# A gate table from one f32r product a token, with its copies and one-hot tiles moved between engines

## The reference

```
u = u_emb[ids]
act = gelu(einsum('ted,td->te', u, xb))
w = gate * act
out = einsum('te,ted->td', w, v_emb[ids])
```

## Time and profile before

| | us |
|---|---|
| median of 3 runs | 3590.15 |
| lowest and highest | 3589.37, 3594.89 |
| the profiled execution's own time | 3598.26 |
| its span in the trace | 3596.5 |

### The profile page before, as it was taken

One profiled execution on the slowest core, in us unless ns is written; L12 is line 12 of the kernel. 1 busy time (PEld: TensorE's weight loads), 2 busy tenths in 40 slices (PEclk: granted clock), 3 DMA queues, 4 the chain that ended last, 5 costly groups with the idle time before them and its releaser, 6 DMA issues. The chain is left out here.

```text
span 3596.5 us, 52641 instructions
## 1 busy us (share of the span) xinstructions
PE 3509.6 (98%) x19484; PEld 2990.6 (83%) x19484; DVE 1772.6 (49%) x3403; ACT 1283.5 (36%) x1851; POOL 500.7 (14%) x428
## 2 busy tenths in 40 slices
PE   8999999999999999999999999999999999899999
PEld 8966787788888878888888899998889789768887
DVE  7344599566665224444444543335445456654333
ACT  4244222466665232222222322233223333333232
POOL 0100125433332001111111010010100000111011
PEclk9989999999999999999999999999999989999999
DMA  4200224355555546666666422222222100122221
GB/s 148 77 18 18 88 95 140 123 175 175 178 181 184 190 144 190 194 189 193 190 193 197 129 88 94 82 94 74 91 85 77 59 1 1 36 76 97 93 99 69
DMA packets 115447, 416.05 MB, mean 116 GB/s; under 512 B 14192, under 2 KB 14320, under 8 KB 113008
## 3 DMA queue, kind: packets, MB, share of 16 engines
q1 hardware_dynamic: 75632, 279.93, 23.6%
q0 software_dynamic: 18944, 67.12, 6.4%
q10 hardware_dynamic: 20736, 67.12, 5.0%
HBM read 344.91 MB, written 69.21 MB: 115 GB/s over the span
## 5 line engine op out<-in xcount | busy, mean ns | idle before, releaser
L447 DVE TENSOR_TENSOR w_lo<-ring,w_hi 128x1024 fp32r<-128x1024 f32 x224 | 275.4, 1230 | 698.0 <-ACT w_hi L443 698.0
L183 DVE TENSOR_TENSOR w_lo<-ring,w_hi 128x1024 fp32r<-128x1024 f32 (+2 forms) x157 | 205.9, 1311 | 568.7 <-ACT w_hi L177 568.7
L443 ACT ACTIVATE w_hi<-ring 128x1024 fp32r<-128x1024 f32 x255 | 270.2, 1059 | 505.9 <-PE ps L493 488.8
L463 PE MATMUL ps<-hn_hi,w_hi 128*128 128x512 f32 x1024 | 408.1, 398 | 3.6 <-POOL w_lo L447 1.4
L463 PE MATMUL ps<-hn_lo,w_hi 128*128 128x512 f32 x1024 | 404.5, 395 | 0.0
L463 PE MATMUL ps<-hn_hi,w_lo 128*128 128x512 f32 x1024 | 402.9, 393 | 0.0
L493 PE MATMUL ps<-units_hi,w_hi 128*128 128x512 f32 x1024 | 399.1, 390 | 2.7 <-DVE units_lo L804 2.7
L493 PE MATMUL ps<-units_hi,w_lo 128*128 128x512 f32 x1024 | 399.0, 390 | 0.0
L493 PE MATMUL ps<-units_lo,w_hi 128*128 128x512 f32 x1024 | 398.9, 390 | 0.0
L177 ACT ACTIVATE w_hi<-ring 128x1024 fp32r<-128x1024 f32 (+2 forms) x170 | 190.2, 1119 | 455.0 <-PE ps L241 381.0
L241 PE MATMUL ps<-f_hn_hi,w_hi 128*128 128x264 f32 (+1 forms) x1056 | 284.6, 324 | 8.9 <-DVE f_hn_lo L855 8.5
(11 more groups left out here) (432 smaller groups left out, 6723.6 us busy)
## 6 DMA issues: line engine op xcount, KB each, us to landing
ring<-in_w_uv SPq DMA_DIRECT2D x256, 512.0 KB, 3.4
ring<-in_f_up SPq DMA_DIRECT2D x88, 512.0 KB, 3.2
expert_units<-scratch ACTq DMA_DIRECT2D x128, 256.0 KB, 2.6
gate_table<-peer ACTq DMA_DIRECT2D x16, 2048.0 KB, 7.2
peer<-gate_table POOLq DMA_DIRECT2D x32, 1024.0 KB, 8.0
peer<-expert_units POOLq DMA_DIRECT2D x128, 256.0 KB, 3.7
ring<-in_w_in SPq DMA_DIRECT2D x29, 512.0 KB, 3.3
ring<-in_w_late SPq DMA_DIRECT2D x25, 512.0 KB, 3.3
```

Of the source, the lines that this page charges most:

```text
L183: self.nc.vector.tensor_tensor(self.l[:, self.slot(k), 0:self.cols], e.ring[:, self.ring(k), 0:self.cols], self.h[:, self.slot(k), 0:self. ...
L443: A_(uh[:, slot(n)], e.ring[:, ring(n), 0:D], ACT.Copy).then_inc(e.hi_done, 1)
L447: ops.tensor_tensor(ul[:, slot(n)], e.ring[:, ring(n), 0:D], uh[:, slot(n)].bitcast(F32), ALU.subtract).then_inc(e.lo_done, 1)
L463: mm = M(e.ps[:, n % 2, :], u[:, slot(n), ch * P:(ch + 1) * P], x[part][:, ch, META:L], start=(ch == 0 and j == 0), stop=(ch == DC - 1 and ...
```

## The change

- **Products.** A token's product becomes one f32r matmul of 256 columns: the moving tile holds the row scaled by the gate's high part and by its low part, side by side. A batch takes two PSUM banks, and two batches alternate (`both`).
- **Rows.** VectorE makes the moving tile by one `scalar_tensor_tensor` of 256 elements a token, from iota, the token's row as a pointer scalar, and the pair of gate parts. It keeps four batches of them.
- **Columns.** GpSimd's `offset` subtracts for every batch; ScalarE's `columns` does Abs and Relu, in place, for every batch, 512 elements each.
- **Evacuation.** ScalarE's `high` copies the half from the high parts out of PSUM, contiguously; VectorE's new `evac` adds the other half from PSUM and writes the transposed table.
- **Order.** `hi` and `lo` are done for unit n+2 in step n. ScalarE: `columns` twice, `gelu`, `spill`, `hi`, `high` twice, and the save every fourth time. VectorE: `hots` for the next step's two batches, `lo`, `evac` twice. In the units 96 to 127, `hi` and `lo` run two ahead as well.
- Once, at the start, the gates are split into their parts. The tiles lie where they did; `tb.high` takes two scratch rows.

```
-    hot, hot_pool, hot_act = e.sem("hot"), e.sem("hot_pool"), e.sem("hot_act")
+    hot, hot_col = e.sem("hot"), e.sem("hot_col")
+    parted, copied = e.sem("gate_parts"), e.sem("high_copied")
...
+    def both(m):
+
+        at = (4 + 2 * (m % 2)) * WIDE
+        return e.psf[:, at:at + 2 * WIDE].rearrange("p (t x i) -> p t x i", t=GT, x=2)
+
...
         def outers(it, m):
 
-            r = m % GR
             pe.wait_ge(hot, it * 16 + (m + 1))
-            if r % 2 == 0:
-                pe.wait_ge(hot_pool, it * 8 + (m // 2 + 1))
-            if r % 4 == 1:
-                pe.wait_ge(hot_act, it * 4 + (m // 4 + 1))
+            pe.wait_ge(hot_col, it * 16 + (m + 1))
             pe.wait_ge(stored, it * 16 + (m + 1))
             for t in range(GT):
-                mm = M(e.ps[:, 4 + m % 4, t * P:(t + 1) * P], tb.cols[:, r, t], tb.rows[:, r, t])
+                mm = M(both(m)[:, t].rearrange("p x i -> p (x i)"), tb.cols[:, m % GR, t],
+                       tb.rows[:, m % 4, t].rearrange("p x i -> p (x i)"))
             mm.then_inc(outer, 1)
...
-        act.sem_inc(stored, 4)
...
         def columns(it, m):
 
-            act.wait_ge(outer, it * 16 + (m + 1))
-            for t in range(GT):
-                col = it * (16 * GT) + (m * GT + t)
-                off = A_(tb.cols[:, m % GR, t], c["iota"], ACT.Abs, bias=e.colT[:, bass.ds(col, 1)], scale=-1.0)
-            off.then_inc(act_offset, 1)
-            act.wait_ge(act_offset, it * 4 + (m // 4 + 1))
-            A_(tb.cols[:, m % GR], tb.cols[:, m % GR], ACT.Relu, bias=e.one, scale=-1.0).then_inc(hot_act, 1)
-
-        def evac(it, m):
-
-            blk = m // BK
-            if m % BK == 0:
-                act.wait_ge(saved[blk], it * 16 + 16)
+            x = tb.cols[:, m % GR]
+            act.wait_ge(pool_offset, it * 16 + (m + 1))
+            A_(x, x.bitcast(F32), ACT.Abs).then_inc(act_offset, 1)
+            act.wait_ge(act_offset, it * 16 + (m + 1))
+            A_(x, x.bitcast(F32), ACT.Relu, bias=e.one, scale=-1.0).then_inc(hot_col, 1)
+
+        def high(it, m):
+
             act.wait_ge(outer, it * 16 + (m + GR + 1))
-            t0 = (m % BK) * GT
-            A_(tb.table[:, blk].rearrange("p i t -> p t i")[:, t0:t0 + GT, :],
-               e.ps[:, 4 + m % 4, :].rearrange("p (t i) -> p t i", t=GT), ACT.Copy).then_inc(stored, 1)
+            A_(tb.high[m % 2], both(m)[:, :, 0], ACT.Copy).then_inc(copied, 1)
 
         def save(it, blk):
 
-            act.wait_ge(stored, it * 16 + (BK * (blk + 1) + 4))
+            act.wait_ge(stored, it * 16 + (BK * (blk + 1) + 2))
             act.dma_start(e.gtab[it * 2 + blk],
                           tb.table[:, blk].rearrange("p i t -> p (i t)")).then_inc(saved[blk], 16)
...
             for j, y in enumerate((e.rowT, e.colT, e.gateT)):
-                cp = A_(y[:, n * P:(n + 1) * P], e.ps[:, 4 + n, j * P:(j + 1) * P], ACT.Copy)
-            cp.then_inc(spread, 1)
+                A_(y[:, n * P:(n + 1) * P], e.ps[:, 4 + n, j * P:(j + 1) * P], ACT.Copy)
+            A_(tb.gates[:, n * P:(n + 1) * P, 0], e.ps[:, 4 + n, 2 * P:3 * P], ACT.Copy).then_inc(spread, 1)
 
         act.wait_ge(spread, nb)
-        columns(0, 1)
-        columns(0, 5)
+        hi(act, 0, 8, AHEAD + 1)
+        for m in range(4):
+            columns(0, m)
 
         def table_step(it, n, more):
-            hi(act, it, 8, AHEAD + n + 1)
+            if more:
+                columns(it, 2 * n + 4)
+                columns(it, 2 * n + 5)
             gelu(it, 8, AHEAD + n)
             spill(it, 8, AHEAD + n - 1)
-            evac(it, 2 * n)
-            evac(it, 2 * n + 1)
-            if n % 2 == 0 and more:
-                columns(it, 2 * n + 1 + GR)
+            hi(act, it, 8, AHEAD + n + 2)
+            high(it, 2 * n)
+            high(it, 2 * n + 1)
             if n % 4 == 3:
                 save(it, n // 4)
 
...
         for n in range(8):
-            table_step(SPREAD // 8 - 1, n, n < 4)
-        with act.Fori(0, REST // 4) as it:
+            table_step(SPREAD // 8 - 1, n, n < 6)
+        with act.Fori(0, REST // 4 - 1) as it:
             for n in range(AHEAD + SPREAD, AHEAD + SPREAD + 4):
-                hi(act, it, 4, n + 1)
                 gelu(it, 4, n)
+                hi(act, it, 4, n + 2)
                 spill(it, 4, n - 1)
+        for n in range(NK - 4, NK):
+            gelu(0, 4, n)
+            if n < NK - 1:
+                hi(act, 0, 4, n + 2)
+            spill(0, 4, n - 1)
         spill(0, 4, NK - 1)
 
...
-        def offset(it, j):
-
-            pool.wait_ge(outer, it * GR + (2 * j + 1))
-            if not isinstance(it, int) or j:
-
-                pool.wait_ge(pool_offset, it * (GR // 2) + j)
-            col = it * (GR * GT) + 2 * j * GT
-            nc.gpsimd.tensor_tensor(tb.cols[:, 2 * j % GR], c["iota"].unsqueeze(1).broadcast_to([P, GT, P]),
-                                    e.colT[:, bass.ds(col, GT)].unsqueeze(2).broadcast_to([P, GT, P]),
+        def offset(it, m):
+
+            pool.wait_ge(outer, it * GR + (m + 1))
+            nc.gpsimd.tensor_tensor(tb.cols[:, m], c["iota"].unsqueeze(1).broadcast_to([P, GT, P]),
+                                    e.colT[:, bass.ds(it * (GR * GT) + m * GT, GT)].unsqueeze(2).broadcast_to([P, GT, P]),
                                     ALU.subtract).then_inc(pool_offset, 1)
 
-        def equal(j):
-            nc.gpsimd.tensor_scalar(tb.cols[:, 2 * j], tb.cols[:, 2 * j], 0.0, None,
-                                    ALU.is_equal).then_inc(hot_pool, 1)
-
-        turns = batches // GR
         pool.wait_ge(spread, nb)
+        with pool.Fori(0, batches // GR) as it:
+            for m in range(GR):
+                offset(it, m)
...
         def hots(it, m):
 
-            r = m % GR
-            dve.wait_ge(outer, it * 16 + (m + 1))
+            dve.wait_ge(outer, it * 16 + (m + GR - 4 + 1))
             for t in range(GT):
                 col = it * (16 * GT) + (m * GT + t)
-                oh = V.tensor_scalar(tb.rows[:, r, t], c["iota"], e.rowT[:, bass.ds(col, 1)],
-                                     e.gateT[:, bass.ds(col, 1)], ALU.is_equal, ALU.mult)
-                if r % 4 == 3:
-                    oh = V.tensor_scalar(tb.cols[:, r, t], c["iota"], e.colT[:, bass.ds(col, 1)], None,
-                                         ALU.is_equal)
+                parts = tb.gates[:, bass.ds(col, 1)].bitcast(F32).rearrange("p o x -> p (o x)")
+                oh = V.scalar_tensor_tensor(out=tb.rows[:, m % 4, t],
+                                            in0=c["iota"].unsqueeze(1).broadcast_to([P, 2, P]),
+                                            scalar=e.rowT[:, bass.ds(col, 1)],
+                                            in1=parts.unsqueeze(2).broadcast_to([P, 2, P]),
+                                            op0=ALU.is_equal, op1=ALU.mult)
             oh.then_inc(hot, 1)
+
+        def evac(it, m):
+
+            blk = m // BK
+            if m % BK == 0:
+                dve.wait_ge(saved[blk], it * 16 + 16)
+            dve.wait_ge(copied, it * 16 + (m + 1))
+            t0 = (m % BK) * GT
+            V.tensor_tensor(tb.table[:, blk].rearrange("p i t -> p t i")[:, t0:t0 + GT, :], tb.high[m % 2],
+                            both(m)[:, :, 1], ALU.add).then_inc(stored, 1)
+
+        def table_step(it, n, more):
+            if more:
+                hots(it, 2 * n + 2)
+                hots(it, 2 * n + 3)
+            lo(dve, V, it, 8, AHEAD + n + 2)
+            evac(it, 2 * n)
+            evac(it, 2 * n + 1)
 
         dve.wait_ge(e.lo_done, base + AHEAD)
         lo(dve, V, 0, 8, AHEAD)
+        lo(dve, V, 0, 8, AHEAD + 1)
+        dve.sem_inc(stored, 2)
         dve.wait_ge(spread, nb)
-        with dve.Fori(0, SPREAD // 8) as it:
+        V.tensor_tensor(tb.gates[:, :, 1], e.gateT, tb.gates[:, :, 0].bitcast(F32), ALU.subtract).then_inc(parted, 1)
+        dve.wait_ge(parted, 1)
+        hots(0, 0)
+        hots(0, 1)
+        with dve.Fori(0, SPREAD // 8 - 1) as it:
             for n in range(8):
-                hots(it, 2 * n)
-                hots(it, 2 * n + 1)
-                lo(dve, V, it, 8, AHEAD + n + 1)
-        with dve.Fori(0, REST // 4) as it:
+                table_step(it, n, True)
+        for n in range(8):
+            table_step(SPREAD // 8 - 1, n, n < 7)
+        with dve.Fori(0, REST // 4 - 1) as it:
             for n in range(AHEAD + SPREAD, AHEAD + SPREAD + 4):
-                lo(dve, V, it, 4, n + 1)
+                lo(dve, V, it, 4, n + 2)
+        for n in range(NK - 4, NK - 1):
+            lo(dve, V, 0, 4, n + 2)
 
         def weigh(it, g):
             q = g // GQ
@@ -2873,7 +2885,11 @@
             k.ranks, k.bits = a.take(4, PH, TOPK), a.take(4, PH, TOPK).bitcast(U32)
             k.tot, k.rec = a.take(nb, PH), a.take(nb, PH)
             a, tb = Arena(region), Env()
-            tb.rows, tb.cols = a.take(GR, GT, P), a.take(GR, GT, P)
+            a.take(2 * GR * GT * P)
```

(34 more changed lines are left out.)

## The result

The changed kernel takes 3638.57 us (median of 4 runs, 3633.37 to 3646.10) where the kernel before takes 3592.22 on the same chip (4 runs, 3589.37 to 3594.89): ratio 1.0127, 95% interval 1.0109 to 1.0145. It is slower, by 46 us where the prediction had 18.

What follows compares the result with a forecast made beforehand. TensorE alone was taken to set the 7.34 us table step; after the change VectorE's 3.14 + 1.14 + 1.36 + 1.74 + 0.25 = 7.63 us would, +18 us over 61 steps: median 3608 us from 3590.15, range 3545 to 3645.

Steps and rivals of the forecast that it cites:

- The forecast: Table stage: VectorE, held up by GpSimd, sets a step of 7.63 us against 7.34, median 3608, own range 3582 to 3632; chance 0.58.
- TensorE's step of 6.53 us: TensorE in a table step: 5.55 us for a plain unit plus 8 f32r products of 0.122, 0.81 less than before.
- One-hot instructions, 0.393 each, and `lo` 1.14: VectorE in a table step: eight one-hot instructions at 0.393 us, 3.14 together, and `lo` at 1.14 as before.
- `evac`, 0.68, from the lower end of 0.60 to 1.0: VectorE's two transposed writes a table step: 0.68 us each, 1.36 together, bounds 0.60 and 1.0 each.
- Rival 3: Transposed write costs VectorE what it costs ScalarE, 1.0 us an `evac`: 8.27 a step, +57, 3647 us; chance 0.15.
- GpSimd puts VectorE back by 0.87 us, twice a step: Table step: each of GpSimd's two subtractions delays VectorE's work by 0.87 us, 1.74 together, bounds 0 and 2.1.
- The turn, 2.0 us of wait, 0.25 a step: Loop turn: VectorE waits 2.0 us for ScalarE's chain behind the save in one step of eight, bounds 0 and 0.5 a step.
- the sum: VectorE's step: 3.14 + 1.14 + 1.36 + 1.74 + 0.25 = 7.63 us against 7.34, in 61 steps +18 us.
- The start, no difference give or take 2: Stage start: ScalarE's six columns precede its first GELU, TensorE waits 1 us; no difference, give or take 2 us.
- Rivals 1 and 2: First: TensorE stays the bound, 6.53 us a step, 3540, chance 0.13; second: one GpSimd turn falls free, 6.76, 3554, 0.14.
- its own sign of being wrong: Changed profile: 6.5 us steps with TensorE never idle, or a GpSimd subtraction beside which a `scalar_tensor_tensor` keeps its length, refute the prediction.
- The shared ports: VectorE and GpSimd: exclusive lock for a whole instruction, needed by VectorE only in two-port mode or with two SBUF inputs; `evac` not held.

## Why the prediction was wrong

The direction was right, and so was the mechanism: VectorE becomes the bound and TensorE's gain is given back whole. The forecast had the largest chance, 0.58, and slower 0.49. The median lies within the range (3545 to 3645), but 30 us above the 3608 predicted, and above the forecast's own 3582 to 3632. By its own steps:

- **TensorE's step of 6.53 us**: 6.51, in every version where nothing else held it. Products are spaced 0.12 apart. Right.
- **One-hot instructions, 0.393 each, and `lo` 1.14**: 0.395 and 1.14. Right.
- **`evac`, 0.68, from the lower end of 0.60 to 1.0**: 0.91. This is the first term that was mis-sized, 0.46 us a step. The reason given, that VectorE's 1.055 ns an element would cover most of a slower write, fell with the run that writes in a row. The 0.4 us more of ScalarE's rows would have been the better guide. Rival 3 had the right cause and somewhat too high a price. The Trainium skill ("SBUF — State Buffer", "Specifications (TRN2)") wants two accesses to an SBUF line of 16 bytes; the run that writes four words at a time and reads in a row, 0.60, agrees with it.
- **GpSimd puts VectorE back by 0.87 us, twice a step**: twice, as predicted, by 0.79 each. It made up 0.16 us of the 0.46. The run with small subtractions shows that it is the cause.
- The step without the turn so becomes 3.16 + 1.14 + 1.82 + 1.58 = 7.70 (7.67 measured) for 7.38 predicted.
- **The turn, 2.0 us of wait, 0.25 a step**: the wait was 3.14, and a turn 3.6 us longer than a step. This is the second mis-sized term: 21.4 us over the six turns, beyond an ordinary step each, where the sum had 15.3. The sum put 6.9 us on ScalarE's chain; it was 7.8, for it left out the 0.9 us from `evac`'s end over the issue of the save to the table load. And VectorE's own work there was 4.65 by the rows and not 4.9. The run with the later save confirms the chain itself.
- **The start, no difference give or take 2**: +5.4 us. This step failed outright. The prediction counted ScalarE's columns, but not that GpSimd, with all eight tiles free, issues nine subtractions without a pause, and that each holds one of VectorE's first instructions. The timelines of GpSimd, VectorE and TensorE at the start of the changed kernel:

```profile
690.75 11.55 POOL L643 TENSOR_TENSOR hot_cols<-const_tab,turned 128x512 fp32r<-128x512 f32 x9 [14.48 <-ACT gate_parts L584]
...
692.79 1.53 DVE L792 TENSOR_TENSOR gate_parts<-turned,gate_parts 128x512 fp32r<-128x512 f32 x1
694.35 12.58 DVE L762 SCALAR_TENSOR_TENSOR hot_rows<-const_tab,turned,gate_parts 128x256 fp32r<-128x256 f32 x16
...
703.03 1.22 PE L479 MATMUL ps<-hot_rows,hot_cols 128*128 128x256 f32 x4 [3.06 <-DVE hot_rows L762]
```

  The split of the gates took 1.53 us, not 0.60, and sixteen one-hot instructions 12.5 us, not 6.3. The prediction had priced the hold for a steady step only.
- **Rivals 1 and 2** (the step stays at 6.53 or near it): they came true for a few steps, 711 to 731 us, where GpSimd was the one held. The prediction took it for given that GpSimd always wins. A subtraction beside which the one-hot instructions keep their length was its own sign of being wrong; there are a few of those (711.48 us, below), and in the other steps the hold came as forecast.
- **The shared ports**: by the Trainium skill ("SBUF — State Buffer", "SBUF: two separate sides") an instruction of VectorE with one input in PSUM needs no lock. The runs agree twice: with the gate parts in PSUM, and with GpSimd beside `evac`.

So the stage grew by 40.6 us where the sum had 18. The 23 or so between them are the start (+5.4), the ordinary step (7.67 for 7.38, +16), the turns (+6), and the six steps at TensorE's pace (-5): the terms that came out too low outweigh those too high.

Of the 46 us in the medians, the two profiled executions show 35. The other 11 are scatter of these two: that of before lies 6.0 us above its median, that of the changed kernel 5.2 below.

## What to carry to other kernels

Before you give VectorE and GpSimd more to do at the same time, write down for every instruction of VectorE whether both its inputs lie in SBUF: those are the ones that a GpSimd instruction puts back by most of its own length, at the start of a stage too, where a free ring lets GpSimd run ahead. They are not the only ones: the kernel before had a `tensor_scalar`, with one tile as input, held as well, 1.15 us for 0.28. Moving one small operand to PSUM, or letting GpSimd go beside instructions that read PSUM, cost nothing that could be seen, and with the save put later turned a loss of 1.3% into gains of 1.4% and 1.3% here. And in a hand-written order don't put a wait for another engine's last result (here a save) ahead of work that this other engine needs next; one step later it was free.

## What the runs showed of the hardware

- **Either engine can be the one that waits.** Timelines of VectorE and GpSimd in an early step of the changed kernel:

```profile
709.88 3.23 DVE L762 SCALAR_TENSOR_TENSOR hot_rows<-const_tab,turned,gate_parts 128x256 fp32r<-128x256 f32 x8
713.02 1.22 DVE L448 TENSOR_TENSOR w_lo<-ring,w_hi 128x1024 fp32r<-128x1024 f32 x1
...
711.48 4.66 POOL L643 TENSOR_TENSOR hot_cols<-const_tab,turned 128x512 fp32r<-128x512 f32 x2 [6.01 <-PE ps L479]
```

  Two subtractions take 4.66 us here (3.66 and 1.04); VectorE's row run and `lo` keep their length, and GpSimd gets through when `evac` begins at 714.16. So GpSimd waited for five instructions of VectorE in a row (four of the one-hot rows and `lo`), not for one, whereas from 731 us on it comes in between two of them. In the changed kernel and four of the versions (in-row evac, later save, runs of four, GpSimd held back at the start), 573 subtractions began while a one-hot instruction ran, and 42 of them took over 1.6 us, 31 of these in the version with runs of four; the longest, 5.16 us, waited for nine instructions. All 42 began 0.01 to 0.39 us behind the start of a one-hot instruction that wasn't itself held, and so did 263 of those that got in. The other 268 began beside an instruction that GpSimd already held, and none of that kind was passed over. What decides in the first case is open; so the pace of such a stage, 6.51 or 7.67 us, is not to be had from durations alone.
- **A write of single words 128 bytes apart** costs VectorE 0.31 us per 512 (the prediction had worked out some 0.4 for ScalarE); in runs of four words it is free, and reads with strides (512 bytes in SBUF, 1 KB in PSUM) cost 0.39.
- **TensorE's clock after a wait.** In the stretch from 900 to 1100 us the granted clock is 0.97 (it was 1.00), and behind the 3.68 us of idle at a turn the unit begins with weight loads of 0.33 us in place of 0.19 (966.80): the granted clock is 0.50 there, the lower of its two levels. The step that follows is 7.60 us, no longer than the others: VectorE sets its pace.
